# A first stage in which each row of K's weights serves three blocks, and V runs seven blocks behind

## The reference, cut to what matters

```python
h = rmsnorm(x, norm_g)
z = h @ w_in                     # columns: q | k | v | f | g_A | u | v_B | g_B
k = z[..., OFF_K:OFF_V]          # 8 heads x 128, also an output
v = z[..., OFF_V:OFF_F]          # 8 heads x 128, also an output
logf = log_sigmoid(z[..., OFF_F:OFF_GA] + b_f)
att = fox_prompt(q, k, v, logf)  # softmax attention with a forget bias (cached keys for samples)
out_b = gmlp_mix(u, layernorm(gelu(v_B)), w_s, b_s) * silu(g_b)
y = x + concat([att * silu(g_a), out_b]) @ w_out
```

## Time and profile before

| what | us |
|---|---|
| median of the runs shown | 1607.96 |
| lowest of the runs shown | 1606.09 |
| the profiled execution, its own time | 1603.71 |
| its span, the slowest core (core 2) | 1600.1 |
| spans of the even cores | 1596.8 to 1600.1 |
| spans of the odd cores | 1561.2 to 1564.7 |
| TensorE busy, of that span | 1515.2 (95%) |

### The profile page before, as it was taken

The page is one execution under the profiler, slowest core; times in us unless marked ns, Lnnn a source line. Parts: engine busy times, 40 slices in busy tenths (PEclk is TensorE's granted clock), DMA queues, the critical chain, the costliest instruction groups (busy, mean ns, idle before and its releaser), DMA issues.

```text
span 1600.1 us, 31906 instructions; the slowest of 8 cores (1561.2 to 1600.1 us)
## 1 busy us (share of the span) xinstructions
PE 1515.2 (95%) x11367; PEld 887.4 (55%) x11367; DVE 600.4 (38%) x1276; ACT 642.5 (40%) x1331; POOL 247.1 (15%) x361
## 2 busy tenths in 40 slices
PE   3899999999999999999989999999999879999998
PEld 1455556554444444444568678677687644444443
DVE  1323222104444023322434445444444534544444
ACT  1222322214565222222227566566565652333332
POOL 5111111140333100000021212221111300000000
PEclk9999999999999999999999999999999899999999
DMA  9965445296000334333398877958846798756752
GB/s 188 232 196 179 178 168 181 109 191 80 1 1 1 40 43 56 44 58 49 50 161 109 117 90 111 116 68 122 102 68 97 122 225 210 226 151 207 188 160 90
DMA packets 266853, 191.38 MB, mean 120 GB/s; under 512 B 224762, under 2 KB 236194, under 8 KB 261634
## 3 DMA queue, kind: packets, MB, share of 16 engines
q1 hardware_dynamic: 125378, 134.69, 30.1%
q0 software_dynamic: 141312, 54.57, 29.7%
HBM read 172.85 MB, written 60.84 MB: 146 GB/s over the span
## 4 chain that ended last, share of the span: by engine, by line
PE 88%; DMA 6%; DVE 1%; ACT 1%; issue 1%; POOL 1%; another core or an unknown queue 0%; SPq 0%; POOLq 0%; DVEq 0%; ACTq 0%
PE psb L581 25%; PE psb L1336 17%; PE psb L785 9%; PE psb L440 8%; PE psb L430 8%; PE psb L945 7%; PE psb L1213 5%; PE psb L1113 5%; DMA arena<-w_in 2%; DMA o_s<-arena 1%; POOL arena L122 1%; PE psb L1133 1%; PE psb L415 1%; DMA arena<-oT_s 1%; DMA arena<-x_own 1%
## 5 line engine op out<-in xcount | busy, mean ns | idle before, releaser
L581 PE MATMUL psb<-arena 128*128 128x496 bf16 (+1 forms) x1920 | 419.1, 372 | 3.2 <-ACT psb L795 2.8
L581 PEld LDWEIGHTS psb<-arena 128*128 128x128 bf16 x1920 | 183.7, 98 | 194.8 <-issue 6.4
L1336 PE MATMUL psb<-arena 128*128 128x512 bf16 (+1 forms) x1280 | 278.7, 381 | 3.7 <-DMA arena<-oT_s 3.7
L1151 ACT ACTIVATE arena<-psb,offb 128x384 bf16<-128x384 f32 x400 | 210.1, 582 | 51.6 <-PE psb L1113 41.2
L945 PE MATMUL psb<-arena 128*128 128x128 bf16 (+1 forms) x2560 | 216.7, 220 | 4.3 <-DVE arena L959 4.3
L1336 PEld LDWEIGHTS psb<-arena 128*128 128x128 bf16 (+1 forms) x1280 | 125.6, 98 | 156.4 <-issue 7.1
L1213 PE MATMUL psb<-arena 128*128 128x129 bf16 x1520 | 176.8, 221 | 14.2 <-DVE arena L1081 7.9
L1113 PE MATMUL psb<-arena 128*128 128x384 bf16 (+3 forms) x552 | 173.7, 315 | 8.1 <-ACT arena L1151 3.7
L945 PEld LDWEIGHTS psb<-arena 128*128 128x128 bf16 (+1 forms) x2560 | 164.0, 98 | 11.9 <-issue 4.4
L430 PE MATMUL psb<-arena 128*128 128x512 bf16 (+1 forms) x640 | 147.4, 389 | 21.8 <-DMA arena<-w_in 15.4
L440 PE MATMUL psb<-arena 128*128 128x344 bf16 (+1 forms) x960 | 146.1, 311 | 7.0 <-DMA arena<-w_in 3.0
(11 more groups left out here) (151 smaller groups left out, 1202.7 us busy)
## 6 DMA issues: line engine op xcount, KB each, us to landing
arena<-x_own SPq DMA_DIRECT2D x38, 1024.0 KB, 6.9
y_own<-arena SPq DMA_DIRECT2D x38, 512.0 KB, 4.7
arena<-w_in POOLq DMA_DIRECT2D x32, 512.0 KB, 6.5
k_own<-arena SPq DMA_DIRECT2D x19, 512.0 KB, 3.7
v_own<-arena SPq DMA_DIRECT2D x19, 512.0 KB, 2.8
arena<-w_in POOLq DMA_DIRECT2D x32, 256.0 KB, 15.7
arena<-ck POOLq DMA_DIRECT2D x16, 512.0 KB, 8.0
arena<-cv POOLq DMA_DIRECT2D x16, 512.0 KB, 8.8
```

What stands on the lines that cost most here:

```text
L581: PE.op(lambda: mm(PSB[bk][:, 0:n], wt[:, k, :], H[:, k, c0:c0 + n], start=(k == 0), stop=(k == KC - 1)), reads=rh + [r_wt], writes=[PSR[b ...
L1151: ACT.op(lambda: act(out=Pb[pi][:, 0:n], in_=PSB[bk][:, 0:n], func=AF.Exp, scale=SCALE, bias=S["offb"][:, t["oo"] + u["g"], h:h + 1]), rea ...
L1336: PE.op(lambda: mm(PSB[bk][0:rows, :], oT[op_][:, k, j * 128:j * 128 + rows], wo[k][:, cg * 512:(cg + 1) * 512], start=(ki == 0), stop=(ki ...
```

## The change

The first three blocks are made together: x blocks 0 to 2 are loaded ahead of everything (three `xbuf`, so that block 3 follows when the first is free), three blocks are normalised and transposed, and then each of the 16 rows of K's weights is multiplied with all three, into banks 2 to 7. The transposes of block 3 come inside this stream, behind row 11. K's weights signal by twos. The three evictions, casts (on VectorE) and stores follow, and the load of x block 4 is issued behind them. For blocks 3 to 6 the transposes of the next block stand inside K's product, behind row 9. V runs seven blocks behind K, so that the first V product comes in turn 7, and eight are left in the last turn. K's f32 stage is `Kf` for even blocks and `Vf` for odd ones as long as V isn't running. ScalarE's table is loaded by a dummy operation at the start. The loads and transposes of W_s move by a few turns and share one place.

```diff
-NPRE = [0, 10]
+NPRE = [0, 8]
...
-        R_WK[k].dsem = mkdsem("wk%d" % (k // 4))
+        R_WK[k].dsem = mkdsem("wk%d" % (k // 2))
...
-    xbuf, R_xbuf = b.many("xbuf", 2, [D], F32)
+    NXB = 3
+    xbuf, R_xbuf = b.many("xbuf", NXB, [D], F32)
...
+    NFIRST = 3
+    LAGV = 7
     a_load(0)
+    load(SP, S["ng16"][:], C.norm_g.rearrange("(k p) -> k p", p=128), R["ng16"])
+    a_load(1)
+    a_load(2)
+    load(SP, S["bfb"][:], C.b_f.partition_broadcast(128), R["bfb"])
+    R_warm = Res("warm")
+    ACT.op(lambda: act(out=S["sml"][:, 60:61], in_=S["ident_f"][:, 0:1], func=AF.Square), reads=[R["ident_f"]], writes=[R_warm])
...
+    def kbank(n, c):
+        return 2 + 2 * n + c if n < NFIRST else 2 + c
...
+    def kstage(n):
+
+        return (Vf, R_Vf) if n < LAGV and n % 2 else (Kf, R_Kf)
...
+    def a_Kcast(n):
+        kind, _, rows = binfo(n)[:3]
+        p = n % 2
+        if kind == "oth":
+            return
+        src, rsrc = kstage(n)
+        if n < NFIRST:
+            DVE.op(lambda: v.tensor_copy(out=Kb[p][0:rows, :], in_=src[0:rows, :]), reads=[rsrc], writes=[R_Kb[p]])
+        else:
+            pool(lambda: g.tensor_copy(out=Kb[p][0:rows, :], in_=src[0:rows, :]), reads=[rsrc], writes=[R_Kb[p]])
...
-    LAGV = 3
-    a_norm(0); a_transp(0)
+    a_norm(0); a_norm(1)
+    a_transp(0)
+    a_norm(2)
+    a_transp(1)
+    a_load(3)
+    a_norm(3)
+    a_transp(2)
+    for k in range(KC):
+        for n in range(NFIRST):
+            for c in range(2):
+                a_Kmm(n, c, k)
+        if k == 11:
+            a_transp(3)
+    for n in range(NFIRST):
+        a_Kev(n, 0); a_Kev(n, 1); a_Kcast(n); a_Kstores(n)
+    a_load(4)
+
     vnext = 0
-    for n in range(NB):
+    for n in range(NFIRST, NB):
         if n + 2 < NB:
             a_load(n + 2)
         if n + 1 < NB:
             a_norm(n + 1)
-        if n == LAGV + 2:
+        if n == LAGV + 1:
             late_setup()
-        a_Kmm(n)
+        for k in range(KC):
+            for c in range(2):
+                a_Kmm(n, c, k)
+            if k == 9 and n < LAGV:
+                a_transp(n + 1)
         if NB - 12 <= n < NB - 12 + npre:
             wvb_load(n - NB + 12)
-        if n == LAGV + 5:
+        if n == LAGV + 3:
             setup_ws()
-        if n + 1 < NB:
+            ws2_rest = setup_ws2() if ns else None
+        if n == LAGV + 5 and ns:
+            ws2_rest()
+        if n >= LAGV and n + 1 < NB:
             a_transp(n + 1)
-        a_Kepi(n)
+        a_Kev(n, 0); a_Kev(n, 1); a_Kcast(n)
```

More of the change, by code:

```diff
@@ L318, in emit @@
     for k in range(KC):
-        R_WK[k].dsem = mkdsem("wk%d" % (k // 4))
+        R_WK[k].dsem = mkdsem("wk%d" % (k // 2))
         R_WV[k].dsem = mkdsem("wv%d" % (k // 4))
-    xbuf, R_xbuf = b.many("xbuf", 2, [D], F32)
-    XB0 = b.off - 16384
+    NXB = 3
+    xbuf, R_xbuf = b.many("xbuf", NXB, [D], F32)
+    XB0 = b.off - NXB * 8192
     xn, R_xn = b.many("xn", 2, [D], BF16)
@@ L353, in a_load @@
         _, _, rows, xsrc, _, _ = binfo(n)
-        load(SP, xbuf[n % 2][0:rows, :], xsrc, R_xbuf[n % 2])
+        load(SP, xbuf[n % NXB][0:rows, :], xsrc, R_xbuf[n % NXB])
+    NFIRST = 3
+    LAGV = 7
     a_load(0)
+    load(SP, S["ng16"][:], C.norm_g.rearrange("(k p) -> k p", p=128), R["ng16"])
[4 more added lines that the diff above has]
+    ACT.op(lambda: act(out=S["sml"][:, 60:61], in_=S["ident_f"][:, 0:1], func=AF.Square), reads=[R["ident_f"]], writes=[R_warm])
     for k in range(KC):
@@ L360, in emit @@
     wsf, R_wsf, _ = place("wsf", b.off, [8, 128], F32)
[L361 to L365, removed]
     def late_setup():
@@ L369, in late_setup @@
             load(SP, S["lfc"][:], C.clf.rearrange("(j p) h -> p j h", p=128), R["lfc"])
[L370 to L373, removed]
         load(SP, wsf[:, :, :], C.w_s.rearrange("g t s -> t g s"), R_wsf)
@@ L401, in a_norm @@
         rows = binfo(n)[2]
-        p = n % 2
+        p, px = n % 2, n % NXB
         ss, sd, rs = [S["sml"][0:rows, p * 4 + i:p * 4 + i + 1] for i in range(3)]
-        ACT.op(lambda: act(out=xn[p][0:rows, :], in_=xbuf[p][0:rows, :], func=AF.Square, accum_out=ss),
-               reads=[R_xbuf[p]], writes=[R_xn[p], R_ss[p]])
+        ACT.op(lambda: act(out=xn[p][0:rows, :], in_=xbuf[px][0:rows, :], func=AF.Square, accum_out=ss),
+               reads=[R_xbuf[px]], writes=[R_xn[p], R_ss[p]])
         ACT.op(lambda: act(out=sd, in_=ss, func=AF.Sqrt, scale=1.0 / D, bias=RMS_EPS), reads=[R_ss[p]], writes=[R_ss[p]])
         DVE.op(lambda: v.reciprocal(out=rs, in_=sd), reads=[R_ss[p]], writes=[R_ss[p]])
-        DVE.op(lambda: v.tensor_scalar(out=xn[p][0:rows, :], in0=xbuf[p][0:rows, :], scalar1=rs, scalar2=None, op0=ALU.mult),
-               reads=[R_xbuf[p], R_ss[p]], writes=[R_xn[p]])
+        DVE.op(lambda: v.tensor_scalar(out=xn[p][0:rows, :], in0=xbuf[px][0:rows, :], scalar1=rs, scalar2=None, op0=ALU.mult),
+               reads=[R_xbuf[px], R_ss[p]], writes=[R_xn[p]])
     def a_transp(n):
@@ L423, in a_transp, with a_Kmm @@
                 reads=[PSR[half], R["gcol"]], pwrites=[rdst])
-    def a_Kmm(n):
+    def kbank(n, c):
+        return 2 + 2 * n + c if n < NFIRST else 2 + c
+    def a_Kmm(n, c, k):
         rows = binfo(n)[2]
         hT, rh = hT_of(n)
[L428 to L433, removed]
+        bk = kbank(n, c)
+        PE.op(lambda: mm(PSB[bk][0:rows, :], hT[:, k, :], WK[:, k, c * 512:(c + 1) * 512], start=(k == 0), stop=(k == KC - 1)),
+              reads=[rh, R_WK[k]], writes=[PSR[bk]] if k == 0 else [], pwrites=[] if k == 0 else [PSR[bk]],
+              sig=(k == KC - 1))
     def a_Vmm(n):
@@ L445, in emit, with a_Kev @@
     VCH = [(0, VC), (VC, VC), (2 * VC, 1024 - 2 * VC)]
-    def a_Kepi(n):
+    def kstage(n):
+        return (Vf, R_Vf) if n < LAGV and n % 2 else (Kf, R_Kf)
+    def a_Kev(n, c):
         kind, _, rows = binfo(n)[:3]
         p = n % 2
[L450 to L459, removed]
+        sl = slice(c * 512, (c + 1) * 512)
+        bk = kbank(n, c)
+        dst, rd = kstage(n) if kind != "oth" else (Kb[p], R_Kb[p])
+        ACT.op(lambda: act(out=dst[0:rows, sl], in_=PSB[bk][0:rows, :], func=AF.Copy),
+               reads=[PSR[bk]], writes=[rd] if c == 0 else [], pwrites=[] if c == 0 else [rd])
+    def a_Kcast(n):
[8 more added lines that the diff above has]
+            pool(lambda: g.tensor_copy(out=Kb[p][0:rows, :], in_=src[0:rows, :]), reads=[rsrc], writes=[R_Kb[p]])
     def a_Vepi(n):
@@ L480, in a_Kstores @@
         if kind != "oth":
-            store(SP, C.k_own[j * 128:(j + 1) * 128, :] if kind == "own" else C.k_smp, Kf[0:rows, :], R_Kf)
+            store(SP, C.k_own[j * 128:(j + 1) * 128, :] if kind == "own" else C.k_smp, kstage(n)[0][0:rows, :], kstage(n)[1])
         store(SP, C.K_s[tcol:tcol + rows, :], Kb[p][0:rows, :], R_Kb[p], R_Ks)
@@ L502, in setup_ws, with setup_ws2, rest @@
                 reads=[PSR[5 + half], R["utri"]], pwrites=[R["WT"]])
-        if ns:
+    def setup_ws2():
+        wsf2, R_wsf2, _ = place("wsf2", b.off, [8, NRMAX], F32)
+        DVE.op(lambda: v.memset(wsf2[0:NR, :, :], 0.0), writes=[R_wsf2])
+        for i in range(ns):
+            pload(SP, wsf2[i * NS:(i + 1) * NS, :, i * NS:(i + 1) * NS], C.w_s[:, 0:NS, 0:NS].rearrange("g t s -> t g s"), R_wsf2,
+                  extra=[R_wsf2])
+        def rest():
             for gi in range(8):
@@ L510, in setup_ws @@
                 reads=[PSR[5], R["utri2"]], writes=[R["WT2"]])
+        return rest
     ring0 = []
@@ L520, in emit @@
     PF = C.asize - npre * 2048
-    assert b.off + 4096 + NRMAX * 32 <= PF
+    assert b.off + 4096 <= PF
     WVB, R_WVB = [None] * KC, [None] * KC
```

## The result

The changed kernel takes 1623.91 us (median), the kernel before 1606.09 beside it, 17.8 us less; the ratio is **1.0117, 95% interval 1.0104 to 1.0130**, which makes 18.8 us. The forecast was 1619 in a range of 1602 to 1634. By the bound of 2% it is no change; by the interval it is a small loss, clear of the noise.

What follows compares the result with a forecast made beforehand. It took transfers to bound the start (47.2 us lost), TensorE the turns after. Start +9.5, tail +3.0, setup -0.6 make 11.9 us on the profiled 1603.7, 1615.6; on runs around 1607.0 it forecast 1619, range 1602 to 1634.

Steps and rivals of the forecast that it cites:

- The three blocks together: At the start, TensorE's stream of 96 matmuls waits until 28.1 us, then ends near 51.5, not held by weights.
- Where it stands next: x block 4: Inside block 3's K, TensorE stops 23 us for block 4's late load; lost time there grows by 9.5 us.
- The tail: At the stage's end eight V's follow one another instead of four; four added at 0.76 us each, +3.0 us.
- Setup of W_s: The split setup of W_s drops its TensorE wait of 0.6 us, and its loads delay only stores with time to spare.
- The sum: Whole kernel: 9.5 + 3.0 - 0.6 = 11.9 us slower; 1615.6 on the profiled execution, 1619 on the lower runs.
- No stop: Block 3's K: block 4 is there by 56 us, so TensorE runs on; 1592 us, chance 0.09.
- Block 4 early: Block 4's load lands at 70.2 because V's weights have mostly passed; 5.1 us less, 1614 us, chance 0.18.
- The stream at the weights' pace: The first three blocks' stream goes at the pace of the weights, ending at 48.4; 3 us less, no chance of its own.
- The disturbed tail: At the stage's end the four added V's cost 2.8 us each, 11.3 instead of 3.0; 1627 us, chance 0.13.
- The lower clock staying: After the 23 us stop TensorE stays at 0.43 us a matmul for blocks 4 to 6; 1642 us, chance 0.04.
- The price of the load: Block 4's 1 MB x load: the skill's fit gives 4.4 us, contradicted by rows of 13.8 and 16.1 beside V's weights.

Runs made afterwards that it cites:

- before_tail: The kernel before with only every second V of its last turn in banks 7, 0 and 1: 1603.9 and 1602.3 us, beside 1602.9 to 1605.8.
- x45_norm: Changed kernel with x blocks 4 and 5 loaded ahead of the stores, plus block 4's norm ahead of block 2's eviction: 1612.31 us, ratio 1.0052.

## Why the prediction was right, point by point

- **The three blocks together.** Right. The stream was to start at 28.1 and did at 28.93; the first store was to go out at 52.1 and went at 52.30. No row of weights was waited for.
- **Where it stands next: x block 4.** The mechanism was right in every step: issue at 64.4 (63.15), landing at 75.3 (77.5), a stop of 23 us (25.4), block 7's K at 112.2 (114.89). The landing was a middle between 70.2 and 80.5 and was 2.2 too early; that is most of why the start cost 12.2 and not 9.5. The load itself took 14.3 us where the middle had 10.9; the issue, 1.25 earlier than forecast, hid a third of that. The cast that was bounded by 0.64 and 1.04 took 0.69.
- **The tail.** Mechanism right, size wrong: 1.40 for each V more, not 0.76, that is 5.6 and not 3.0 us. The row chosen, 344.40 to 352.16, was the last V's; behind it comes the next stage, which needs other banks and doesn't wait, so it hides half of the price. The hole of 0.57 that the prediction gives as the reason stands ahead of 344.40, outside the 7.76. The disturbed V's beside it were rightly left out: in the change too only two of the eight are disturbed.
- **Setup of W_s.** Right: from 125 to 400 us TensorE waits for nothing but the V's in a row and 0.2 us.
- **The sum.** 12.2 + 5.6 - 0.6 = 17.2 us, where 11.9 were forecast. In the two profiled executions the next stage starts 369.72 - 352.16 = 17.6 us later, so the terms account for the stage. The spans differ by 19.6: the other 2.0 come behind the stage, for which core 0 takes 1250.0 us, core 2 of the same execution, from 369.09 on, 1246.1, and core 2 of the kernel before 1247.9. Why the even cores differ there is open. Both terms, the start (9.5) and the tail (3.0), were too small, so the forecast owes nothing to errors that cancel but the 1.25 us of the issue.
- **The rivals.** No stop: out. Block 4 early: out, it landed nearer to the late bound. The stream at the weights' pace: out, it waits for no row. The disturbed tail: out for the change, though before_tail shows its mechanism alive in the kernel before. The lower clock staying: out. Windows of the changed kernel (busy times; then granted clock, DMA share, GB/s):

```profile
68.00:76.00 8.00, 0.00 (x0) 0.00 (x0) 0.00 (x0) 0.00 (x0) 0.00 (x0) 0.50 1.04 253
...
84.00:92.00 8.00, 6.70 (x29) 2.83 (x29) 2.73 (x4) 3.18 (x5) 1.04 (x1) 0.95 0.34 116
92.00:100.00 8.00, 7.10 (x44) 3.48 (x44) 2.84 (x5) 3.18 (x5) 1.04 (x1) 1.00 0.51 202
```

The clock stands at half, the 1.2 GHz level, while TensorE stops, and is back to the full one within the first K after it. The Trainium skill (TensorE: Matmul & The Clock Gate, HAM oscillation) has the products behind such a wait start at the lower clock; the rows agree, 11 matmuls in 3.31 us after the stop against 2.75 later.

- **The price of the load.** The changed kernel's loads of x, issued at 63.1 to 63.6 and at 89.9 to 90.4 (size, time to landing):

```profile
arena<-x_own SPq DMA_DIRECT2D x1, 1024.0 KB, 14.3
```

```profile
arena<-x_own SPq DMA_DIRECT2D x1, 1024.0 KB, 5.1
```

The 4.4 us estimated from the Trainium skill (DMA: Bandwidth & Descriptors, Anatomy of one DMA), by a fit for GpSimd's path, come near to a load once V's weights are through, 5.1; beside them the measurement, 14.3, decides.

What the prediction didn't see: that the lag costs as much where there is no such stop. It priced the lag in the tail and saw that V "could use this time", but made block 4's place on SP the cause. Against the kernel before, the new start at lag 3 costs 0.3%, the old start at lag 7 1.1%, and the new start at lag 7 1.2%. So nearly all of the loss comes with the lag, whichever start stands ahead of it: V no longer fills what TensorE would wait for, the stop on block 4 in the new start, the holes of 2.27 in the old one, and the tail grows. The three-block stream saves the 15.4 us of waits for weights and pays them back in the stop. At lag 7, too, early loads or the other banks each bring back more than half of the loss.

The expectation of x45_norm also missed something: the store behind the 10.1 us that the early loads left went on to hold TensorE through VectorE.

## What to carry to other kernels

A start that is fed by transfers is won by what TensorE can do with what has landed, so look at who is next once the new work is through: here a load, behind three stores on the same queue, behind an eviction that waited for the first of them. A load without a dependence of its own belongs ahead of stores that have one. Work that lags fills the stops of the work ahead; before making a lag longer, count which stops it filled, and price its tail by a row in the middle of a run, not by the last one.

## What the runs showed that I had not expected

- The same half megabyte of store took 7.4 to 10.9 us beside the weights and 2.6 to 5.9 between 88 and 300 us, and with one f32 stage that, not the bytes, paced a whole chain over ScalarE, VectorE and SP.
- Matmuls went at the 1.2 GHz pace (eight in 3.57 us) in stretches in which the granted clock reads 1.00 as well as in one in which it reads 0.52; the pace of the matmuls is the safer reading. The former, a window of the kernel before:

```profile
20.45:24.00 3.55, 3.55 (x8) 0.99 (x8) 0.00 (x0) 0.00 (x0) 3.55 (x8) 1.00 1.06 191
```

- VectorE casts 128 x 1024 elements from f32 to bf16 in 0.69 us, GpSimd in 1.04.
